# A two-layer hybrid decoder trunk: the next layer's first four products each ahead of a tile's turns

## What is computed

```
for l in range(2):
    h = rmsnorm(x, norm_mix[l])
    proj = h @ w_in[l]                 # 1024 x 3184, feeds four head groups
    heads = concat(ssd(..), dsa(..), mla(..), fox(..))
    x = x + heads @ w_out[l]
    h2 = rmsnorm(x, norm_ffn[l])
    x = x + hier_moe(h2, ..)           # 32 experts, two for each token
return rmsnorm(x, final_norm)
```

## Time and profile before

| what | value |
|---|---|
| median of 3 runs | 2775.8 us (2769.75 to 2779.78) |
| profiled execution, its time | 2776.44 us |
| its span | 2774.7 us |
| TensorE (PE) busy | 2470.2 us, 89% |
| VectorE (DVE) busy | 1196.3 us, 43% |
| ScalarE (ACT) busy | 912.7 us, 33% |
| mean granted clock of TensorE | 0.948 |

### The profile page before, as it was taken

The page is one execution under the profiler, slowest core; times in us unless marked ns, Lnnn a source line. Parts: engine busy times, 40 slices in busy tenths (PEclk is TensorE's granted clock), DMA queues, the critical chain, the costliest instruction groups (busy, mean ns, idle before and its releaser), DMA issues.

```text
span 2774.7 us, 30141 instructions
## 1 busy us (share of the span) xinstructions
PE 2470.2 (89%) x10358; PEld 1398.0 (50%) x10374; DVE 1196.3 (43%) x2732; ACT 912.7 (33%) x1882; POOL 187.7 (7%) x370
## 2 busy tenths in 40 slices
PE   6999789789999689999689996997899995999994
PEld 3565334556654444444345642455566553444442
DVE  3434478865531421111333426789555224111115
ACT  2131379554531111111122215784545111111113
POOL 0000031000000010000200001310000000000002
PEclk9999999999999789999889999999999996999996
DMA  6100001301000569999511001013010015899975
GB/s 235 43 31 25 31 13 55 115 2 46 1 11 31 219 228 358 367 370 365 197 54 48 10 25 34 22 56 103 1 46 1 10 46 227 318 359 370 368 294 204
DMA packets 105712, 370.54 MB, mean 134 GB/s; under 512 B 20758, under 2 KB 40172, under 8 KB 81004
## 3 DMA queue, kind: packets, MB, share of 16 engines
q1 hardware_dynamic: 91760, 318.54, 32.0%
q0 software_dynamic: 13824, 50.34, 4.8%
HBM read 304.42 MB, written 64.30 MB: 133 GB/s over the span
## 4 chain that ended last, share of the span: by engine, by line
PE 70%; DVE 14%; issue 7%; ACT 6%; DMA 1%; PEldq 1%; PEld 1%; POOL 0%; DVEq 0%; ACTq 0%; SPq 0%; POOLq 0%
PE bank L1163 16%; PE bank L755 10%; PE bank L1180 8%; PE bank L1111 8%; PE bank L835 5%; PE bank L744 5%; PE bank L758 5%; PE bank L867 4%; ACT group_arena L1438 2%; ACT heads_cols L1430 2%; PE bank L1038 1%; PE bank L1124 1%; DVE softmax_stats L1733 1%; PE bank L1149 1%; DVE residual L2222 1%
## 5 line engine op out<-in xcount | busy, mean ns | idle before, releaser
L755 PE MATMUL bank<-w_ring,normed_cols 128*128 128x260 f32 (+4 forms) x1280 | 432.8, 490 | 5.0 <-ACT heads_cols L1463 3.2
L755 PEld LDWEIGHTS bank<-w_ring,normed_cols 128*128 128x128 f32 x1280 | 237.0, 191 | 172.7 <-issue 154.1
L758 PE MATMUL bank<-normed_cols,w_ring 128*128 128x512 f32 x640 | 284.4, 604 | 7.4 <-ACT group_arena L1340 6.5
L744 PE MATMUL bank<-ident,group_arena 128*128 128x128 f32 (+1 forms) x1200 | 187.3, 299 | 112.0 <-DVE group_arena L1661 86.4
L1180 PE MATMUL bank<-heads_cols,group_arena 128*128 128x512 f32 x512 | 231.8, 595 | 2.8 <-DVE group_arena L2182 2.8
L1163 PE MATMUL bank<-w_ring,group_arena 128*128 128x512 f32 x512 | 231.1, 605 | 3.3 <-issue 1.7
L744 PEld LDWEIGHTS bank<-ident,group_arena 128*128 128x128 f32 (+1 forms) x1200 | 144.3, 151 | 165.9 <-issue 90.0
L1163 PE MATMUL bank<-normed_cols,group_arena 128*128 128x512 f32 x512 | 224.9, 592 | 0.0
L1111 PE MATMUL bank<-w_ring,heads_cols 128*128 128x512 f32 x512 | 222.6, 594 | 2.0 <-DVEq L252 2.0
L758 PEld LDWEIGHTS bank<-normed_cols,w_ring 128*128 128x128 f32 x640 | 122.8, 194 | 161.5 <-issue 152.9
L2182 DVE COPY group_arena<-bank 128x256 f32<-128x256 f32 x64 | 27.1, 424 | 395.4 <-PE bank L1170 395.4
(11 more groups left out here) (322 smaller groups left out, 3063.3 us busy)
## 6 DMA issues: line engine op xcount, KB each, us to landing
heads_cols<-in_expert_w_down SPq DMA_DIRECT2D x64, 1024.0 KB, 9.0
w_ring<-in_expert_w_gate SPq DMA_DIRECT2D x32, 1024.0 KB, 10.0
w_ring<-in_expert_w_up SPq DMA_DIRECT2D x32, 1024.0 KB, 14.6
normed_cols<-in_expert_w_gate SPq DMA_DIRECT2D x32, 1024.0 KB, 10.3
normed_cols<-in_expert_w_up SPq DMA_DIRECT2D x32, 1024.0 KB, 15.0
expert_rows<-group_arena SPq DMA_DIRECT2D x64, 512.0 KB, 9.2
w_ring<-in_w_in SPq DMA_DIRECT2D x6, 2048.0 KB, 9.1
expert_rows<-heads_cols SPq DMA_DIRECT2D x1, 8192.0 KB, 27.7
```

The costliest lines, as they stand in the source:

```text
L744: last = pe.transpose(bank(4 + r % 2)[0:rows, col:col + src.shape[0]], src, ident[0:src.shape[0], 0:src.shape[0]])
L755: m = pe.matmul(out[:, 0:width], HT[:, k, part * P:(part + 1) * P], w, start=(k == 0), stop=(k == K - 1))
L758: m = pe.matmul(out[0:width, :], w, HT[:, k, part * HALF:(part + 1) * HALF], start=(k == 0), stop=(k == K - 1))
```

## The change

Products 0 to 3 now each stand ahead of the wait and the turns of tiles 4 to 7. Product 0 reads what the turns of tiles 0 to 3 left in `HT`, so ahead of it TensorE waits for the eviction of the last two turns.

```diff
             def turn_normed(first, then=lambda n: None):
 
                 for t in range(T):
+                    if t == T // 2:
+                        for r in (tr.n - 2, tr.n - 1):
+                            pe.wait_ge(tr_taken[r % 2], r // 2 + 1)
+                    if t >= T // 2:
+                        then(t - T // 2)
                     pe.wait_ge(rows_normed, first + t + 1)
                     for b in range(0, K, 4):
                         turn([(i * P, P, normed[:, t, (b + i) * P:(b + i + 1) * P]) for i in range(4)])
-                    if t >= T // 2:
-                        then(t - T // 2)
```

## The result

The changed kernel took 2783.26 us (median of 11 runs, 2776.58 to 2785.54) against 2775.8 us for the kernel before in 11 runs beside it (2769.37 to 2780.62). The two medians are 7.5 us apart. The ratio estimated from all single runs is 1.0023, with a 95% interval of 1.0013 to 1.0033: +6.4 us, between 3.6 and 9.2. It is slower, by less than the 0.3% that the prediction took as the bound of a change, and the median lies above the range forecast. Run again beside other kernels it was at 1.0020 (1.0010 to 1.0029).

What follows compares the result with a forecast made beforehand. The prediction took TensorE to bound most of the program. Set-up -0.05 us and layer change -0.18 us, together -0.2, took the median from 2775.8 to 2775.6 us, with a range of 2770.5 to 2781.5.

Steps and rivals of the forecast that it cites:

- Step 1: Start of product 0: 0 us in the set-up; -0.15 us at the layer change (ends -0.6 and +3.0).
- rival C: At the layer change product 0's compare-and-branch is bared, costing up to 3.63 us; total 2778.8 us, chance 0.09.
- Step 2: Turn 4 runs at the full clock in set-up and layer change: -0.86 and -0.89 us, or 0 at the other end.
- Step 3: The last turn's evictions lose product 3's cover: +0.81 us in the set-up, +0.86 us at the layer change.
- Steps 4 and 5: Later evictions and norms have slack, and the last layer's moved branches hide beside norm waits or evictions: 0 us each.
- Rival A: Full clock lost at the first loop head by a 3.05 us product-to-product pause: +2.15 us, 2777.8 us, chance 0.30.
- D: Something the examined places don't show, such as the length of cold stretches elsewhere: either way, chance 0.06.

Runs made afterwards that it cites:

- the change again: The changed kernel, unaltered, run once more against the kernel before: ratio 1.0020 (1.0010 to 1.0029), +5.5 us.
- order before, same instructions: Changed kernel's text with a switch set to the old order in both places, instruction for instruction the kernel before: ratio 1.0000 against it, 0 us.
- product 3 behind: Changed kernel with product 3 put back behind tile 7's turns (both places: +3.3, again +2.5 us; set-up only: +1.1 us), against the kernel before.
- the filler that kept the clock: Changed kernel plus one useless 128x512 matmul behind tile 7's turns in the set-up: ratio 1.0011 to the kernel before, +3.1 us.
- The measured cost of the layer's end: Changed order at the layer's end only, set-up as in the kernel before: ratio 1.0013 (1.0004 to 1.0022) to that kernel, +3.6 us.

## Why the prediction was wrong

*Step 1, the start.* Right in the set-up: product 0 started at 33.06 for the 32.82 forecast, and at 33.61 to 33.65 in the six other profiles with this set-up, where turn 4 in the old order started at 33.7 in five of seven. At the layer change the wait, branch and first product cost 0.76 us, in place of the 0.45 taken; in the profile of the change again product 0 began at 1396.05 behind an eviction that ended at 1393.64 + 1.06 = 1394.70, so 1.35. Turn 4 had come 1394.60 - 1394.00 = 0.60 us behind those evictions, so product 0 starts 0.2 and 0.75 us later behind them, not 0.15 earlier. That is well short of the 3.63 of rival C.

*Step 2, the warm turn,* is the first step that failed. Turn 4 ran in 0.87 us, as forecast, but the 0.86 and 0.89 us booked for it were not gained. The step dated the clock's rise 4.2 to 4.4 us behind the first product, from three places of one profile, and so held product 0's cold part fixed. Those three agreed by luck. In the fourteen profiles the rise comes 1.0 to 4.3 us behind the first product in the old order and 3.5 to 6.2 in the new, in the set-up and at the layer change alike. Counted from the first work of the run, transposition or product, it is 2.7 to 6.1 and 3.5 to 6.2 us. At the layer change of "order before, same instructions" TensorE's timeline reads

```profile
1392.74 1.97 PE L744 MATMUL bank<-ident,group_arena 128*128 128x128 f32 x8 [2.90 <-DVE group_arena L1666]
1394.50 7.61 PE L758 MATMUL bank<-normed_cols,w_ring 128*128 128x512 f32 x16
```

and product 0 takes 7.61 us there, where the prediction's profile had 9.18. Product 0 put ahead takes over the cold time that turn 4 had. That is the other end which the step named (0 us), and the set-ups with product 3 behind bear it out: 0.4 us later in the mean, not 0.86 earlier.

*Step 3, the uncovered evictions.* Right in kind, somewhat less in size: from the turn's start at 65.77 to the end of ScalarE's last eviction at 66.84 + 0.60 = 67.44 it is 1.67 us, where 1.68 was taken. From the start of the last pair of turn and product to the loop's first product it is 68.85 - 58.90 = 9.95 us, against 68.27 - 58.99 = 9.28 before, in which the turn comes first: +0.67 us for the 0.81 taken.

*Steps 4 and 5.* Right. TensorE waits for no norm between the products, and the last layer's turns start where the norms end.

*Rival A,* which had a chance of 0.30, came true: the full clock is lost at the first head, in three profiles of three. From product to product the pause is 68.85 - 65.77 = 3.08 us, as worked out (3.05). The price was 8.82 - 7.13 = 1.7 us, not 2.15. With the 0.67 us of step 3 it makes 2.4 of the 2.8 us that the set-up costs in the mean; the other 0.4 lies within the scatter of the set-ups (1.7 us among those in the old order). The Trainium skill, "TensorE: Matmul & The Clock Gate", Part 4, says that a transposition doesn't count as a busy TensorE in the same way; the trace agrees with the outcome, but doesn't prove that reading, since even with the turn counted the pause had grown from 1.37 to 2.04 us, and the filler that kept the clock cut it to 1.4. The rises of the other profiles, just given, don't bear it out either. The prediction had set against this rival that 2.6 us without work was the shortest pause that cost the clock. It had looked at two places only: in the same profile TensorE paused 2.20 us ahead of the SSD part's first small product at 1526.37, and the clock fell at 1527.0.

*The step that was missing* is the cost of untouched code, which stood only in D, "something these places don't show", with 0.06. At the layer change the clock is lost in either order, so the code behind it was costed at nothing because no instruction of it moved. What moved was its distance from the clock's next fall. 1.6 us of that is seen directly, the longer entry of layer 1's SSD part, in each of the six profiles with the long stretch. Over the whole of layer 1 those six average 1295.4 us from the third product to the last layer's first turn, the eight others 1293.0, and of these the six without fillers 1291.5. The measured cost of the layer's end, +3.6 us, is then 0.7 at the head, 1.6 at the entry, and 1.3 that lies within its interval; whether further stretches of layer 1 carry it stays open.

*The sum,* -0.2 us, is so replaced by about 2.8 at the first head, 0.7 at the second and 1.6 at the entry, 5.1 us, beside +5.5 and +6.4 measured. This adds up parts of single profiles and is an estimate.

*The range* was too narrow for A and the entry at once. It held each loss by itself.

## What to carry to other kernels

Work moved ahead of a pause takes the cover from whatever now stands last, and a pause that was just short enough to keep TensorE's clock can become too long: sum the pause from product to product, in both readings of what counts. And where the clock falls and rises behind pauses, a shift of half a microsecond ahead of them is not neutral for the code behind; costing untouched code at zero is right only to within what such a stretch costs, here 1.6 us. A time read at three places of one profile is not fixed because the three agree: the cold part of product 0 was, over fourteen profiles, anything from 1.0 to 6.2 us. For changes of this size, a control of the same instructions and both halves run apart say more than the two profiles, which differed by 6.3 us, 4.4 of it in a part where executions of the old order differ as much among themselves.

## What the runs showed of the hardware

- A cold stretch at the start of layer 1's SSD part lasted either 3.4 or 6.8 us in all fourteen profiles. Which of the two went by the distance of the loop's third product from the clock's last rise, with the change between 12.78 and 12.87 us. The fall itself came 88.7 us after that rise in all of them, wherever the work stood.
- At the start of a run of work the clock rose 1.0 to 6.2 us behind the first product and 2.7 to 6.2 us behind the first work of either kind, in executions of the same instructions too (first product: 4.3 and 1.15 us at the layer change of the kernel before and of its control).
- A pause of 3.08 us from product to product, with a 0.87 us turn at its start, cost the full clock in three profiles of three; a pause of 1.4 us kept it.
- One 128x512 matmul (0.87 us) of no use at the layer change made the kernel before 3.1 us slower (0.3 to 5.8) and turned the stretch from 3.4 to 6.8 us, and the same matmul in the set-up took the changed kernel from +5.5 and +6.4 us to +3.1 (intervals that overlap), with the third product of the loop at 83.57 us in place of 85.06.
- From the end of the evictions that it waited for to the first matmul, TensorE with a wait and a compare-and-branch took 0.76 and 1.35 us, in two executions of the same kernel.
